# A decoder layer on one core: second feed-forward with seven block products per tile, its weight sums added by GpSimd during the first

## The reference

```python
h = x + 0.5 * swiglu(rms(x), w_ffn1_in, w_ffn1_out)          # first feed-forward, hidden width 2816
u, q, k, v, qi, ki, wi, gs, ga = split(rms(h) @ w_in)
s5  = glu(gelu(ssm(u)))                                       # complex diagonal state space, 32 groups
att = sparse_top_k_attention(q, k, v, qi, ki, wi)             # prompt and paged sample keys
h = h + (sigmoid(gs) * s5 + sigmoid(ga) * (att @ w_att)) @ w_out
h = h + 0.5 * swiglu(rms(h), w_ffn2_in, w_ffn2_out)          # second feed-forward
y = rms(h)                     # swiglu(n, a, b): gate, up = split(n @ a); (silu(gate) * up) @ b
```

## Time and profile before

| what | us |
|---|---|
| median of 3 runs | 1456.93 |
| lowest, highest run | 1445.45, 1458.88 |
| the profiled execution: span from the first to the last instruction | 1450.0 |
| TensorE busy | 1376.6 |
| VectorE busy | 654.6 |
| ScalarE busy | 495.6 |
| GpSimd busy | 265.2 |

### The profile page before, as it was taken

How to read it: one execution, slowest core, us unless ns; L and a number is a source line. 1 busy time by engine, 2 the same in 40 slices (tenths; PEclk the granted TensorE clock), 3 DMA queues, 4 the chain that set the end, 5 groups by cost and what they waited for, 6 DMA issues and landing times.

```text
span 1450.0 us, 28752 instructions
## 1 busy us (share of the span) xinstructions
PE 1376.6 (95%) x11422; PEld 1289.9 (89%) x11422; DVE 654.6 (45%) x1093; ACT 495.6 (34%) x720; POOL 265.2 (18%) x325
## 2 busy tenths in 40 slices
PE   6999999999999899997999888899999999999996
PEld 5999999999987678875999777689999999999996
DVE  4333333434352226975987423245533443343344
ACT  5332222212232221244877432332432222222234
POOL 4000000288205002022667422100000000000000
PEclk9999999999997999999999999999999999999998
DMA  9522232333234363234222669663233322233221
GB/s 135 154 82 87 80 89 87 90 90 89 66 108 67 81 88 98 49 109 77 73 59 85 216 213 348 200 209 88 73 102 87 87 88 87 87 87 88 80 66 62
DMA packets 228818, 152.62 MB, mean 105 GB/s; under 512 B 27425, under 2 KB 209833, under 8 KB 228730
## 3 DMA queue, kind: packets, MB, share of 16 engines
q1 hardware_dynamic: 200512, 121.07, 28.9%
q0 software_dynamic: 7728, 19.97, 5.6%
q10 hardware_dynamic: 20490, 10.36, 3.3%
HBM read 141.85 MB, written 8.34 MB: 104 GB/s over the span
## 4 chain that ended last, share of the span: by engine, by line
PE 90%; DVE 3%; ACT 3%; issue 2%; DMA 1%; SPq 1%; ACTq 0%; DVEq 0%
PE ps L642 58%; PE ps L622 9%; PE ps L1036 3%; PE ps L1052 3%; PE ps L1153 3%; PE ps L1122 2%; PE ps L1205 1%; DVE uv L2139 1%; PE ps L1184 1%; PE ps L819 1%; PE ps L1067 1%; PE ps L926 1%; PE ps L1076 1%; PE ps L922 1%; PE ps L807 0%
## 5 line engine op out<-in xcount | busy, mean ns | idle before, releaser
L1778 DVE TENSOR_TENSOR w_low<-wraw,w_high 128x1024 fp32r<-128x1024 f32 x144 | 179.5, 1247 | 319.1 <-ACT w_high L1268 319.1
L1268 ACT ACTIVATE w_high<-wraw 128x1024 fp32r<-128x1024 f32 x144 | 152.6, 1060 | 443.3 <-PE ps L642 438.8
L642 PE MATMUL ps<-hn_high,w_high 128*128 128x272 f32 x1408 | 292.1, 289 | 2.9 <-DVE w_low L1778 2.9
L642 PE MATMUL ps<-hn_high,w_low 128*128 128x272 f32 x1408 | 291.9, 289 | 0.0
L642 PE MATMUL ps<-hn_low,w_high 128*128 128x272 f32 x1408 | 290.7, 288 | 0.0
L642 PEld LDWEIGHTS ps<-hn_high,w_high 128*128 128x128 f32 x1408 | 222.2, 189 | 3.1 <-issue 3.0
L642 PEld LDWEIGHTS ps<-hn_low,w_high 128*128 128x128 f32 x1408 | 221.8, 189 | 0.0
L642 PEld LDWEIGHTS ps<-hn_high,w_low 128*128 128x128 f32 x1408 | 220.2, 189 | 0.0
L642 PE MATMUL ps<-act_high,w_high 128*128 128x272 f32 x832 | 173.1, 289 | 3.4 <-DVE act_low L1778 1.9
L642 PE MATMUL ps<-act_high,w_low 128*128 128x272 f32 x832 | 172.0, 288 | 0.0
L642 PE MATMUL ps<-act_low,w_high 128*128 128x272 f32 x832 | 171.7, 288 | 0.0
(11 more groups left out here) (364 smaller groups left out, 1801.0 us busy)
## 6 DMA issues: line engine op xcount, KB each, us to landing
wraw<-in_w_ffn_in SPq DMA_DIRECT2D x88, 512.0 KB, 3.9
wraw<-in_w_ffn_out SPq DMA_DIRECT2D x32, 512.0 KB, 3.8
wslot<-in_w_in SPq DMA_DIRECT2D x16, 512.0 KB, 3.8
wraw<-in_w_ffn_out SPq DMA_DIRECT2D x16, 384.0 KB, 3.4
wslot<-in_w_in SPq DMA_DIRECT2D x4, 1024.0 KB, 5.6
wslot<-in_w_s_glu SPq DMA_DIRECT2D x16, 256.0 KB, 3.0
biasmem<-in_cache_k SPq DMA_DIRECT2D x16, 256.0 KB, 4.4
biasmem<-in_cache_k POOLq DMA_DIRECT2D x16, 256.0 KB, 5.1
```

The costliest lines, as they stand in the source:

```text
L642: ins = pe.matmul(ps[:, bank + h, 0:HALF], a[:, w_at, k, :], x[:, lo_at(k) if x is x_lo else k, h * HALF:(h + 1) * HALF], start=(k == 0 an ...
L1268: act_e.activation(wh[:, j % 2, :, :], wraw[:, j, :, :], ACT.Copy).then_inc(s["hi_done"], 1)
L1778: return dve.tensor_tensor(o, a, b, op)
```

## The change

A tile of the second feed-forward is a product of a 2 x 2 block matrix of weights (gate and up columns by two halves of the inner dimension, 512 each) with a 2 x 2 block matrix of activations (the halves of the inner dimension by the two token halves). Before, it is computed as eight block products. The change computes seven, each 4 blocks x 3 terms = 12 matmuls, from three weight blocks as they are and four sums of blocks, and from seven activation blocks, four of them sums.

- GpSimd makes the four weight sums of each of the 22 column tiles: it loads four blocks of 256 KB, adds four times, and stores the sums to a DRAM scratch (`scr_w`). That starts after the second unit of the first feed-forward and stands ahead of the S5 matrices, whose two loops are written out. The load of `ohs` moves behind the S5 matrices, since part of its room holds sums. The last output part of the first feed-forward waits on VectorE for the stores (`sums_out`).
- SP loads seven blocks per tile (three of `w_ffn2_in`, four of `scr_w`) into two sets of raw buffers.
- ScalarE rounds and VectorE splits them in pairs of products, three pairs and one single. During the `w_out` units both make the seven activation blocks, high and low.
- Four products have a bank of their own, three add to a bank that holds another. ScalarE copies the first product out, and VectorE forms gate and up from the banks with seven operations of 272 columns in place of one scaling by 544. The output units are as before.

```diff
--- before.py
+++ after.py
+            sums_odd = over.enter_context(nc.sbuf_tensor("sums_odd", [P, 2, 4, P], F32))
...
+            sums_even = over.enter_context(nc.sbuf_tensor("sums_even", [P, 4, 4, P], F32))
...
+            xc_low = rounded(over, "xc_low", [P, 7, 4, HALF])
+            more_high = rounded(over, "more_high", [P, 3, 4, P])
+            more_low = rounded(over, "more_low", [P, 3, 4, P])
+            wfront = over.enter_context(nc.sbuf_tensor("wfront", [P, 7, 4, P], F32))
...
+        scr_w = nc.dram_tensor("scr_w", [4, FK, P, 4, P], F32, kind="Internal").ap()
...
+        XC = (0, 1, 4, 5, 2, 3, 6)
+        BANK = (0, 1, 2, 3, 0, 1, 3)
...
+            def piece(f, p):
+                if p in (0, 4, 6):
+                    c0, k0 = P * f + (FF if p == 6 else 0), 4 if p else 0
+                    return w_in[:, k0:k0 + 4, c0:c0 + P]
+                return scr_w[(None, 0, 1, 2, None, 3)[p], f]
+            def load_pair(g, f, q):
+                for p in range(2 * q, min(2 * q + 2, 7)):
+                    sp.dma_start(raw_slot(f, p), piece(f, p)).then_inc(raw_sem(f, q), 16)
+            def load_out(g, f0, m, j):
+                sp.dma_start(wraw[:, j % 4, 0:m, :], w_out[:, f0:f0 + m, P * j:P * j + P]).then_inc(raw_in[j % 4], 16)
+            sp.wait_ge(s["att_mm"], DK)
+            sp.wait_ge(s["sums_out"], 64 * FK)
+            for q in range(4):
+                load_pair(0, 0, q)
+            for q in range(4):
+                sp.wait_ge(s["lo_done"], FE0 + FFN_UNITS + 5 + q)
+                load_pair(0, 1, q)
...
+            def product(f, p, high_ready, low_ready, block_wait=None):
+                pe.wait_ge(s["hi_done"], high_ready)
+                order = (0, 2, 1) if block_wait is not None else (0, 1, 2)
+                for n in order:
+                    a, x = ((high_slot(p), xc_high), (high_slot(p), xc_low), (low_slot(p), xc_high))[n]
+                    if n == 2:
+                        pe.wait_ge(s["lo_done"], low_ready)
+                    for k in range(4):
+                        if block_wait is not None and n < 2:
+                            block_wait(n, k)
+                        ins = pe.matmul(bank_of(f, p), a[:, k, :], x[:, XC[p], k, :], start=(n == 0 and k == 0 and p < 4),
+                                        stop=(n == order[2] and k == 3), skip_group_check=True)
+                ins.then_inc(s["unit_done"], 1)
+            def fused_tile(g, f, r=None):
+                def at(value, step):
+                    return value if r is None else r * (2 * step) + value
+                for p in range(7):
+                    if p == 0 and f < 2 and r is None:
+                        pe.wait_ge(s["ffn_ev"], FE0 + FFN_TILES + 7 + f)
+                    elif p == 0:
+                        pe.wait_ge(s["combined"], at(combined_at(f - 2, "up0"), 7))
+                        if r is None and f < GROUPS[g][0] + 2:
+                            pe.wait_ge(s["out_scaled"], DK * g - 1 + f % 2)
+                    if p == 4:
+                        pe.wait_ge(s["first_out"], at(f + 1, 1))
+                    if p == 2 and f == 1 and r is None:
+                        pe.wait_ge(s["sqrt_done"], 2)
+                    if p == 5:
+                        pe.wait_ge(s["combined"], at(combined_at(f, "v"), 7))
+                    if p == 6:
+                        pe.wait_ge(s["combined"], at(combined_at(f, "up1"), 7))
+                    split = split_at(g, f, p // 2) if r is None else U1 + 4 * f + DK * g + p // 2 + 1
+                    product(f, p, at(split, 4), at(FE0 + split, 4), first_blocks(p) if f == 0 and r is None else None)
+                    if f == 0 and p == 3 and r is None:
+                        norm_sum(2, 6)
...
+            def tile_high_pair(g, f, q):
+                act_e.wait_ge(raw_sem(f, q), raw_tile_at(g, f, q))
+                if f > GROUPS[g][0] or (g and q >= 2):
+                    act_e.wait_ge(s["unit_done"], product_at(f_group(f - 1), f - 1, min(2 * q + 1, 6)))
+                elif g:
+                    act_e.wait_ge(s["unit_done"], product_at(g, f, 0) - 2 + q)
+                elif q < 3:
+                    act_e.wait_ge(s["unit_done"], U1 - (1, 2, 0)[q])
+                act_e.activation(high_pair(q), raw_pair(f, q), ACT.Copy).then_inc(s["hi_done"], 1)
+            def first_out(g, f):
+                act_e.wait_ge(s["unit_done"], product_at(g, f, 0))
+                act_e.activation(mid[:, 0, :], bank_of(f, 0), ACT.Copy).then_inc(s["first_out"], 1)
...
-            pool.dma_start(ohs[:], t["oh_sample"]).then_inc(s["par_in"], 16)
-            pool.wait_ge(s["s5_scalars"], 2)
-            pool.wait_ge(s["early_act"], 1)
...
+            def sum_loads(c):
+                if c:
+                    pool.wait_ge(s["sums_in"], 64 * c)
+                if c >= 2:
+                    pool.wait_ge(s["sums_out"], 64 * (c - 1))
+                for n, piece in enumerate((lift(0, c), lift(1, c), gate(0, c), gate(1, c))):
+                    pool.dma_start(sum_part(c, n), piece).then_inc(s["sums_in"], 16)
+            def weight_sums(c):
+                pool.wait_ge(s["sums_in"], 64 * (c + 1))
+                l0, l1, g0, g1 = [sum_part(c, n) for n in range(4)]
+                pool.tensor_tensor(l1, l0, l1, ALU.add).then_inc(s["sums_done"], 1)
+                pool.tensor_tensor(l0, l0, g0, ALU.add).then_inc(s["sums_done"], 1)
+                pool.wait_ge(s["sums_done"], 4 * c + 1)
+                pool.tensor_tensor(g0, g0, l1, ALU.add).then_inc(s["sums_done"], 1)
+                pool.wait_ge(s["sums_done"], 4 * c + 3)
+                pool.tensor_tensor(g1, g1, g0, ALU.add).then_inc(s["sums_done"], 1)
+            def sum_stores(c):
+                pool.wait_ge(s["sums_done"], 4 * c + 4)
+                for n in range(4):
+                    pool.dma_start(scr_w[(2, 0, 1, 3)[n], c], sum_part(c, n)).then_inc(s["sums_out"], 16)
+            pool.wait_ge(s["unit_done"], 2)
...
-            with pool.Fori(0, 9) as k:
-                product(0, k, power(k, 0), power(k, 1), cT[:, 0], cT[:, 1], at_lag(yre, k), at_lag(yim, k), ALU.add, ALU.subtract)
-            with pool.Fori(0, CH) as k:
-                product(54, k, power(k * -1 + 7, 0), power(k * -1 + 7, 1), bbar[:, 0], bbar[:, 1],
+            def lag_product(k, at):
+                product(6 * at, 0, power(k, 0), power(k, 1), cT[:, 0], cT[:, 1], at_lag(yre, k), at_lag(yim, k), ALU.add, ALU.subtract)
+            def step_product(k, at):
+                product(6 * at, 0, power(7 - k, 0), power(7 - k, 1), bbar[:, 0], bbar[:, 1],
                         at_lag(wb[:, 0], k), at_lag(wb[:, 1], k), ALU.subtract, ALU.add)
+            sum_loads(0)
+            for c in range(FK):
+                if c < FK - 1:
+                    sum_loads(c + 1)
+                weight_sums(c)
+                sum_stores(c)
+            pool.wait_ge(s["s5_scalars"], 2)
+            pool.wait_ge(s["early_act"], 1)
+            for k in range(9):
+                lag_product(k, k)
+            for k in range(CH):
+                step_product(k, 9 + k)
             pool.sem_inc(s["prep_done"], 1)
+            pool.wait_ge(s["par_in"], 16 * PARAMS)
+            pool.wait_ge(s["sums_out"], 64 * FK)
+            pool.dma_start(ohs[:], t["oh_sample"]).then_inc(s["par_in"], 16)
...
+            def cross_sums(j):
+                dve.wait_ge(s["x_scaled"], X0 + j + 1)
+                if j < 4:
+                    tt(xdiff[:, j, :], side(xs_block(j), 0), side(xs_block(j), 1), ALU.subtract).then_inc(s["sums_done"], 1)
+                    return
+                c = cross(j - 4)
+                dve.wait_ge(s["sums_done"], 4 * FK + j - 3)
+                link(tt(c[:, 0, :], side(xs_block(j), 1), xdiff[:, j - 4, :], ALU.add))
+                tt(c[:, 1, :], side(xs_block(j - 4), 1), side(xs_block(j), 1), ALU.subtract)
+                tt(c[:, 2, :], side(xs_block(j), 0), c[:, 0, :], ALU.subtract).then_inc(s["sums_done"], 1)
...
+            def combine(g, f):
+                dve.wait_ge(s["unit_done"], product_at(g, f, 2))
+                dve.wait_ge(s["first_out"], f + 1)
+                tt(mid[:, 1, :], bank_of(f, 2), mid[:, 0, :], ALU.subtract).then_inc(s["combined"], 1)
+                dve.wait_ge(s["combined"], combined_at(f, "u"))
+                tt(mid[:, 2, :], mid[:, 1, :], bank_of(f, 1), ALU.subtract).then_inc(s["combined"], 1)
+            def combine_up1(g, f):
+                dve.wait_ge(s["unit_done"], product_at(g, f, 3))
+                dve.wait_ge(s["combined"], combined_at(f, "v"))
+                tt(side(up, 1), mid[:, 2, :], bank_of(f, 3), ALU.add).then_inc(s["combined"], 1)
+            def combine_gate(g, f):
+                dve.wait_ge(s["unit_done"], product_at(g, f, 4))
+                tt(side(sg[:, f % 2, :], 0), bank_of(f, 4), side(rstd, 0), ALU.mult).then_inc(s["combined"], 1)
+                dve.wait_ge(s["unit_done"], product_at(g, f, 5))
```

(60 more changed lines are left out.)

512 lines of the change are left out of this document (369 added, 143 removed).

## The result

Changed kernel: median **1466.17 us** (8 runs, 1463.64 to 1476.32); kernel before, beside it, 1450.38 us (8 runs, 1442.55 to 1458.88). Ratio 1.012, 95% interval 1.009 to 1.015: slower by 1.2%. Run again among the experiments, 1463.93 us (10 runs) against 1453.56 (13 runs): 1.0069, 1.0038 to 1.0100. The forecast was 1447 us, faster; the time lies inside the range, on the other side of "before".

The account below looks back on a forecast made before the run. TensorE was taken as the bound, with 90% of the chain of waits. From the median of 1456.9 us, -33.1 + 5 + 17.7 + 1 = -9.4 gave 1447 us (chance 0.52), range 1425 to 1480.

Parts of the forecast that it names:

- The products and the start: Second feed-forward: 84 matmuls a tile in place of 96, -33.1 us, and thin covers at its start, +5.
- The start's part of it: Tiles 0 and 1 of the second feed-forward: late cross sums lose 1 us, the reciprocal about 4; +5 (0 to 8).
- Lateness of the S5 matrices: Behind 22 GpSimd rounds of 14.8 us, matrices ready at 453.9 against 436.2, holding TensorE: +17.7 us.
- wait for stores: In each GpSimd round, before the next loads: taken as 3.0 us, between 2.6 and 5.2.
- Rival 2: Stores at 5.2 us make GpSimd's rounds 17.0; S5 matrices 62 us late, 1492 us; chance 0.14.
- The first feed-forward: First round's sum loads fall in the crowded stretch before 50 us, where a weight load already came late: +1 (0 to 3).
- The middle: From the first S5 transpose to the second feed-forward's first product; the prediction's sum had no term for it.
- the short gaps: Sign foreseen in the changed profile: two short gaps of TensorE in tiles 0 and 1 of the second feed-forward.
- Slower by 1%: Outcome passed from a GpSimd round of 16.0 us; most of rivals 2 and 3, chance 0.19.

Follow-up runs that it names:

- e2_sums_of_one_tile: Changed kernel with GpSimd forming only tile 0's sums, read by every tile (output not the reference's): 1424.24 us, 0.982 of the kernel before.
- e9_changed_again: The changed kernel once more, unedited, traced a second time: 1463.93 us (10 runs).
- e1_adds_before_loads: Changed kernel with a tile's four GpSimd adds put ahead of the loads of the next tile: 1429.97 us, 0.986 of the kernel before.
- e6_wait_alone: On top of e1_adds_before_loads, 48 idle GpSimd products between the last S5 matrix and the signal to TensorE: 1459.08 us.
- e4_matrices_between_rounds: Changed kernel with two S5 products behind the stores in each of GpSimd's last 8 rounds: 1457.03 us, 1.005 of the kernel before.

## Why the prediction was wrong

The forecast summed -33.1 + 5 + 17.7 + 1. Term by term:

- **The products and the start, -28.1**: right. 27.4 us (417.3 to 389.9), and 27.5 in e2_sums_of_one_tile. The tiles are 10.5 us apart (three weight roundings of ScalarE, each the first of its tile):

```profile
1106.37 1.06 ACT L1537 ACTIVATE w_high<-wraw 128x1024 fp32r<-128x1024 f32 x1 [0.89 <-PE ps L908]
...
1116.91 1.06 ACT L1537 ACTIVATE w_high<-wfront 128x1024 fp32r<-128x1024 f32 x1 [0.89 <-PE ps L908]
...
1127.46 1.06 ACT L1537 ACTIVATE w_high<-wraw 128x1024 fp32r<-128x1024 f32 x1 [0.89 <-PE ps L908]
```

- **The start's part of it, +5**: right, 4.1 us in four waits of TensorE in tiles 0 and 1, the largest on the copy of tile 1's first product, which stood behind the reciprocal as foreseen:

```profile
PE ps L908 <- ACT mid L1546: 2.2, 1, 2.2
PE ps L908 <- ACT xc_high L1526: 1.3, 1, 1.3
PE ps L908 <- DVE mid L2139: 0.4, 1, 0.4
PE ps L908 <- DVE w_low L2139: 0.2, 1, 0.2
```

- **Lateness of the S5 matrices, +17.7**: the mechanism was right, the size was 31.2. The term that failed is the **wait for stores**, "The weight loads of this stage hold 0.29 of the engines, so I take 3.0, near the lower end". It took 4.4. An average share was read as if it lay under each store. The 0.29 is made of single loads, mostly of 512 KB, and in half the rounds one was issued beside the stores: those waits are 5.2 us, the forecast's own upper figure. The others are 3.6, not 3.0; in nearly every round 0.6 us of the wait lies between the landing of the last store and the next load, which the sum did not have. Rival 2 had the long price, but gave it to every round and put it down to the sums' own 2 MB, whose loads had landed by then. The rest of the round came out: loads 3.0 (3.0 foreseen), adds 6.1 with 0.3 behind them (6.7), stores 2.2 (2.1); sum 16.06 against 14.8. Twenty rounds are 25 us; the first stores were out at 59.3, not 62.0, so the sums ended 22.8 us later than forecast (389.4). The matrices took 81.6 us, not 87.3, and TensorE came 3.7 us later than 436.2: 17.7 + 22.8 - 5.7 - 3.7 = 31.1.
- **The first feed-forward, +1**: 3.8. 3.1 us of it are TensorE's waits for VectorE, whose splits run beside GpSimd's adds. In the changed kernel up to 440 us they are:

```profile
PE ps L814 <- DVE w_low L2139: 3.7, 3, 2.9
...
PE ps L802 <- DVE rstd L2139: 3.0, 1, 3.0
...
PE ps L814 <- DVE act_low L2139: 2.4, 2, 1.2
```

  9.1 us, where the kernel before and e2_sums_of_one_tile have 6.0 (2.9, 2.3 and 0.8). In e9_changed_again, with the same arrival, they make 7.4, so the rest has another cause, which stays open. In e1_adds_before_loads they make 11.0, and the clock comes on top: from 40 to 60 us the granted clock was 0.91 there and 1.00 in e6_wait_alone, the same code up to the last S5 matrix, which arrives 2.1 us earlier.
- **The middle** stood at zero; in the first trace it is +6.7, with a lower granted clock, and +0.4 in the second. What part of it belongs to the changed kernel is not shown.

That 1466 lies inside the stated range is in part luck. The sum was taken from 1456.93, the median of three runs of the kernel before; that of eight is 1450.38, and from there the same terms give 1441.

By the statement of what would show it: the short gaps and the 10.5 us are there, the wait is there with 31 in place of 18, and the rounds are nearer 17 than 14.8. "Slower by 1%" was placed at a round of 16.0, and it is 16.06. The choice of one term at its lower end turned the sign: 31 us is inside the forecast's own bounds of lateness (5 to 34), but at their far end, since 1.4 us on one wait becomes 28 us when it is queued twenty times ahead of the critical chain.

## What to carry to other kernels

A cost on an idle engine is free only up to the moment somebody waits for what stands behind it: multiply the uncertainty of one round by the number of rounds before calling the slack enough. Do not price a DMA wait by the average share of the engines: ask which single transfers can be issued beside it, and how often (here 5.2 us in half the rounds and 3.6 in the others, at a share of 0.29 before). In a round of load, work and store with two buffers, put the work between the stores and the loads that reuse their buffer; and before filling a wait with other work, list all appointments of what is pushed back, since e4_matrices_between_rounds lost at the second one what it won at the first.

## What the runs showed of the hardware

- A GpSimd add of 128x512 takes 1.26 to 1.32 us in 60 of the changed kernel's 88; the other 28, mostly one a round, take 1.45 to 2.3. While TensorE and VectorE stood (453 to 471 us of the changed kernel), an S5 product took 3.9 us from start to start; beside VectorE's splits in e1_adds_before_loads 3.9 to 5.9. The lone ones:

```profile
459.36 2.35 POOL L2027 TENSOR_TENSOR kvtok<-qkT,kis 128x256 f32<-128x256 f32 x4
...
463.27 2.35 POOL L2027 TENSOR_TENSOR kvtok<-qkT,kis 128x256 f32<-128x256 f32 x4
```

  The Trainium skill (SBUF — State Buffer, Who interferes with whom) says that such instructions of the two engines shut each other out for a whole instruction. The trace agrees: each of the 28 long adds began while VectorE was in a split with two inputs in SBUF, and is longer by up to 1.0 us.
- Two executions of the changed kernel differ by 6 us in the same stage (603.4 and 597.1), with the granted clock at other levels in the same work (0.83 and 0.91 from 360 to 400 us behind the first transpose). A difference of 0.4% read from two single traces would have been put down to the change.
